# Channel sums of a head pair as f32r passes over high and low halves

## The chip, the cores and the metric

The kernel runs on one core of a Trainium2 chip. The metric is the device time of one execution in microseconds (us); three executions of the kernel before gave 2422.89, 2422.91 and 2429.49 us.

## What is computed

Two layers run one after the other on 256 positions of 2048 channels: a block with a pooling, a long-convolution and a gating mixer and a feed-forward part, and a hybrid layer of banded attention, a recurrent state layer and memory attention. The change lies in the hybrid layer, in sums over channels. Cut to those:

```python
# recurrent layer: 16 heads of 64 channels
kk = heads(k * f(k_k))
kk = kk * lax.rsqrt(jnp.maximum(jnp.sum(kk * kk, axis=-1, keepdims=True), 1e-24))   # keys
...
o = rwkv7_scan(rh, dh, kh, vh, -kk, kk * ah)
mean = jnp.mean(o, axis=-1, keepdims=True)
var = jnp.mean(jnp.square(o - mean), axis=-1, keepdims=True)                         # outputs
o = ((o - mean) * lax.rsqrt(var + GN_EPS)).reshape(bsz, s, B_WIDTH) * f(ln_w) + f(ln_b)
bonus = jnp.sum(rh * kh * f(r_k), axis=-1, keepdims=True) * vh                       # bonus
# banded attention: 8 heads of 128 channels
aq = rms_norm(aq.reshape(bsz, s, A_HEADS, A_HEAD_DIM), a_q_g)                        # queries
ak = rms_norm(ak.reshape(bsz, s, A_HEADS, A_HEAD_DIM), a_k_g)
```

## The kernel before

Activations lie transposed, with channels on the 128 partitions and the 256 positions along the free side. All large weights come as one stream of 736 **units** of 512 KB, through a ring of four buffers. SP loads a unit into `raw`; ACT copies it, rounded to f32r, into `w_hi` (L967, a wait on `unit_used` for the slot, which TensorE gives four units later); DVE writes the rest `raw - w_hi` into `w_lo` (L1391); TensorE (PE) then runs the 24 products of the unit (`unit`, or `part` in this stage): for each of 4 contraction tiles and 2 output tiles `w_hi` by `h_hi`, `w_hi` by `h_lo`, `w_lo` by `h_hi`, each 128x128 by 256 columns. ACT and DVE run their program four units ahead of PE: `units(k)` on them splits the unit that PE will use at `k + 4`. So "PE's unit k" below is the one in `units(k)` of PE, and "the split of k" is what ACT and DVE do in theirs.

The stage that the change touches has eight rounds, one for each group of two recurrent heads and one attention head (a "head pair" below), 16 units a round. In each round PE weaves two things between its units: `heads(k, g)`, which prepares the pair g from the 16 units' results, and `late`, which works off the pair before (a triangular inverse by chunks of 64, four chunk states one after the other, the attention). The first 16 units run `heads` alone, with work of their own (DVE's six `prefix` steps); then a loop of seven iterations runs `late` with `heads`; then `late` runs once more with the queries of the next stage. The order of each engine is written out by hand, and an engine takes its instructions strictly in that order; semaphores with counts tie them.

The sums over channels are products by a matrix of ones on PE in fp32, from buffers of 128x256 fp32 numbers:

- keys and bonus: DVE squares the keys into `sq` and multiplies `rk` at its split of 6 (`keys_ready`); PE multiplies both by `head_ones` behind its unit 9 into bank 7 (`head_sums`); DVE reads them at its split of 9.
- queries and keys of attention: ACT squares bank 0 into `qr` at its split of 11; PE multiplies `qr` (512 columns) by `ones` behind unit 12; ACT takes the root at its split of 12 (L1214).
- outputs: ACT squares the centred outputs into `gsq`; PE multiplies by `head_ones` behind unit 11; ACT takes the root into `groot`, DVE inverts it (L1994) before its split of 12.

Of DVE in `late`, this stretch matters: it writes the state of chunk 2 (`S`), then does the split of 8 with what `heads` has at 8 (`t0`, `k0`, `v`), then the solution `SA` of chunk 3. At the start of the next `late`: the split of 0, eight masked copies, the reciprocal of `qr` (L1908), `qk` (for PE, which multiplies `qk` behind its unit 1).

Of the kernel before, what the change touches and what calls it, by code (L numbers as in the profile page):

```python
# [26 lines left out]
P = 128  # L27
# [140 lines left out]
def build(nc, a):  # L168
    out_ap = a["out"]
    with ExitStack() as ctx:  # L170
# [100 lines left out]
        for n, w in (("pr", 257), ("pk", 257), ("pv", 257), ("t0", 256), ("r", 256), ("k0", 256), ("v", 256),  # L271
                     ("k2", 256), ("kk", 256), ("sq", 256), ("rk", 256), ("bz", 256), ("ep", 260), ("en", 256),
                     ("a_rt", 512)):
            small[n] = place("s_" + n, [P, w], at)
# [79 lines left out]
        free_mem = sem("free_mem")  # L354
        keys_ready = sem("keys_ready")
        head_sums = sem("head_sums")
# [9 lines left out]

        PROJ = [banks[0], banks[1], banks[3], banks[4]]
# [55 lines left out]
        def _(pe):  # L423
# [51 lines left out]
            pe.wait_ge(tab_in, 32)  # L475
            norm_sums(acc)
# [185 lines left out]

            def heads(k, half=None):

                part(k, half)
                if k == 9 and half != 0:
                    pe.wait_ge(keys_ready, n.next("keys"))
                    mm(banks[7][:, 0:T], con_("head_ones"), small["sq"][:, :])
                    mm(banks[7][:, T:2 * T], con_("head_ones"), small["rk"][:, :]).then_inc(head_sums, 1)
                if k == 12:  # L670
                    pe.wait_ge(sums_read, n.next("sums"))
                    pe.wait_ge(qk_squared, n.next("qk"))
                    mm(banks[7][:, :], con_("ones"), qr[:, :, :].rearrange("p s t -> p (s t)")).then_inc(qk_sums, 1)

            def late(units):
# [283 lines left out]
        def _(act):  # L959
# [57 lines left out]
            act.wait_ge(tab_in, 32)  # L1017
            act.activation(spare[:, 0:1], con_("eps6"), ACT.Sqrt)
# [174 lines left out]
            def heads(k, g):  # L1193
# [15 lines left out]
                if k == 11:  # L1209
                    act.activation(qr[:, :, :], p2(0), ACT.Square).then_inc(qk_squared, 1)  # L1210
                    copy(qk[:, :, :], p2(0)).then_inc(bank_read[0], 1)
                if k == 12:
                    act.wait_ge(qk_sums, n.next("qk"))
                    to_dve(act.activation(flat(qr), banks[7][:, :], ACT.Sqrt, bias=con_("eps6"), scale=1.0 / P))  # L1214
                if k == 13:
# [3 lines left out]
                    to_dve(act.activation(small["en"][:, :], cg_, ACT.Exp, scale=rate))  # L1219
                if k == 15:  # L1220
# [12 lines left out]
            def late(units):  # L1233
# [43 lines left out]
                for k in range(12, 16):  # L1277
                    units(k)
# [965 lines left out]
```

## Time and profile before

| what | value |
|---|---|
| median of three runs | 2422.91 us |
| the profiled execution, its own time | 2422.74 us |
| its span, first to last instruction | 2421.0 us |
| PE busy | 2354.3 us, 97% |
| PE weight loads busy | 2295.7 us, 95% |
| DVE busy | 1507.5 us, 62% |
| ACT busy | 1104.7 us, 46% |
| one iteration of the loop of seven | 70.3 us (1410.90 to 1481.20, say) |
| mean granted clock of TensorE | 0.992 |

The profiled execution lies 0.17 us below the median, and 1.7 us of it are outside the span. Each engine's timeline gives start, duration, line, operation and tiles of every instruction, and in brackets how long the engine was idle before it and who ended that. Starts of matmuls are the pace; their durations overlap, so a matmul of 0.28 us may be followed by the next 0.12 us later. In the profile `s_t` is `t0`, `s_k` is `k0` or `k2`, `con` holds the matrices of ones.

### The profile page before, as it was taken

How to read it: one execution, taken by the hardware profiler on the slowest of the kernel's cores; microseconds unless marked ns; L12 is line 12 of the kernel's file. 1: busy time of each engine (PE TensorE's matmuls, PEld its weight loads, DVE VectorE, ACT ScalarE, POOL GpSimd, SP SyncE). 2: the span in 40 equal slices, each digit the busy share in tenths (PEclk: the TensorE clock that was granted, in tenths of full speed). 3: DMA queues.
4: the chain of work that ended last, by engine and by line, in shares of the span. 5: the costliest groups of instructions: out<-in, count | busy, mean ns of one | idle time of the engine just before them, and what ended most of it. 6: DMA issues, size and time to landing. Idle time of an engine off the chain costs nothing.

```text
span 2421.0 us, 54358 instructions
## 1 busy us (share of the span) xinstructions
PE 2354.3 (97%) x21920; PEld 2295.7 (95%) x21920; DVE 1507.5 (62%) x2072; ACT 1104.7 (46%) x1455; POOL 12.8 (1%) x27
## 2 busy tenths in 40 slices
PE   6999999999999999997999999999999999999999
PEld 6898999999999999996899999999989999999999
DVE  6456776666546667667866666776576554555554
ACT  5343445555434555434444444444465444444442
POOL 0000000000000000000000000000000000000000
PEclk9999999999999999998999999999999999999999
DMA  6453555555555555554343334333445365555554
GB/s 231 141 183 114 174 182 188 186 189 185 189 190 186 190 186 186 188 185 143 126 132 109 126 117 135 126 126 128 149 161 170 111 206 186 189 189 185 192 185 162
DMA packets 110235, 401.34 MB, mean 166 GB/s; under 512 B 12378, under 2 KB 12405, under 8 KB 109952
## 3 DMA queue, kind: packets, MB, share of 16 engines
q1 hardware_dynamic: 108000, 390.91, 49.1%
q0 software_dynamic: 2080, 8.06, 1.0%
q8 instruction: 136, 2.23, 0.4%
q14 instruction: 19, 0.16, 0.0%
HBM read 396.81 MB, written 2.10 MB: 165 GB/s over the span
## 4 chain that ended last, share of the span: by engine, by line
PE 93%; DVE 4%; ACT 1%; issue 1%; DMA 0%; DVEq 0%; SPq 0%; ACTq 0%
PE bank L428 93%; ACT w_hi L967 1%; DVE scratch L1440 1%; DVE w_lo L1391 1%; DVE s_k L1440 0%; DMA x<-in_xT 0%; DVE h_lo L1437 0%; DVE cum L1437 0%; DVE S L1443 0%; PE bank L742 0%; DVE ping L1437 0%; DVE s_t L1437 0%; DVE root L1479 0%; DVE acc L1437 0%; PE bank L691 0%
## 5 line engine op out<-in xcount | busy, mean ns | idle before, releaser
L1391 DVE TENSOR_TENSOR w_lo<-raw,w_hi 128x1024 fp32r<-128x1024 f32 x736 | 896.8, 1224 | 783.2 <-ACT w_hi L967 777.9
L967 ACT ACTIVATE w_hi<-raw 128x1024 fp32r<-128x1024 f32 x736 | 778.3, 1060 | 1088.7 <-PE bank L428 1076.5
L428 PE MATMUL bank<-h_hi,w_hi 128*128 128x256 f32 x4016 | 1149.6, 286 | 19.4 <-issue 8.3
L428 PE MATMUL bank<-h_lo,w_hi 128*128 128x256 f32 x4016 | 1125.6, 280 | 0.0
L428 PE MATMUL bank<-h_hi,w_lo 128*128 128x256 f32 x4016 | 1124.2, 280 | 0.0
L428 PEld LDWEIGHTS bank<-h_hi,w_hi 128*128 128x128 f32 x4016 | 759.3, 189 | 34.1 <-issue 14.3
L428 PEld LDWEIGHTS bank<-h_lo,w_hi 128*128 128x128 f32 x4016 | 759.6, 189 | 3.2 <-issue 2.2
L428 PEld LDWEIGHTS bank<-h_hi,w_lo 128*128 128x128 f32 x4016 | 759.1, 189 | 0.0
L428 PE MATMUL bank<-m_hi,w_hi 128*128 128x256 f32 x704 | 196.5, 279 | 0.0
L428 PE MATMUL bank<-m_lo,w_hi 128*128 128x256 f32 x704 | 196.5, 279 | 0.0
L428 PE MATMUL bank<-m_hi,w_lo 128*128 128x256 f32 x704 | 196.5, 279 | 0.0
L428 PEld LDWEIGHTS bank<-m_hi,w_hi 128*128 128x128 f32 x704 | 132.3, 188 | 0.0
L428 PEld LDWEIGHTS bank<-m_lo,w_hi 128*128 128x128 f32 x704 | 132.3, 188 | 0.0
L428 PEld LDWEIGHTS bank<-m_hi,w_lo 128*128 128x128 f32 x704 | 132.3, 188 | 0.0
L428 PE MATMUL bank<-ya_hi,w_hi 128*128 128x256 f32 x384 | 107.1, 279 | 0.0
L428 PE MATMUL bank<-ya_lo,w_hi 128*128 128x256 f32 x384 | 107.1, 279 | 0.0
L428 PE MATMUL bank<-ya_hi,w_lo 128*128 128x256 f32 x384 | 107.1, 279 | 0.0
L1440 DVE SCALAR_TENSOR_TENSOR conv_o<-scaled_up,par,conv_o 128x255 f32<-128x255 f32 x176 | 77.1, 480 | 6.2 <-DVE conv_o L1440 5.9
L428 PE MATMUL bank<-mh_hi,w_hi 128*128 128x256 f32 x256 | 73.8, 288 | 5.4 <-DVE mh_lo L1437 3.4
L428 PEld LDWEIGHTS bank<-ya_hi,w_hi 128*128 128x128 f32 x384 | 72.2, 188 | 0.0
L428 PEld LDWEIGHTS bank<-ya_lo,w_hi 128*128 128x128 f32 x384 | 72.2, 188 | 0.0
L428 PEld LDWEIGHTS bank<-ya_hi,w_lo 128*128 128x128 f32 x384 | 72.2, 188 | 0.0
(404 smaller groups left out, 2712.3 us busy)
## 6 DMA issues: line engine op xcount, KB each, us to landing
raw<-in_units SPq DMA_DIRECT2D x736, 512.0 KB, 3.8
x<-in_xT SPq DMA_DIRECT2D x4, 512.0 KB, 6.0
memx<-in_memT POOLq DMA_DIRECT2D x4, 512.0 KB, 7.9
out_y<-obuf SPq DMA_DIRECT2D x8, 256.0 KB, 4.5
bias_t<-in_bias POOLq DMA_DIRECT2D x8, 192.0 KB, 3.2
dft<-in_dft POOLq DMA_DIRECT2D x1, 1024.0 KB, 7.7
decay<-in_decay POOLq DMA_DIRECT2D x1, 768.0 KB, 5.8
inv<-in_inv POOLq DMA_DIRECT2D x1, 512.0 KB, 3.8
```

Source lines behind the costliest of these rows:

```text
L428: return pe.matmul(out, lhsT, rhs, start=start, stop=stop, skip_group_check=True)
L967: return act.activation(out, in_, ACT.Copy, scale=scale)
L1391: dve.tensor_tensor(w_lo[slot][:, :, :], raw[slot][:, :, :], w_hi[slot][:, :, :].bitcast(F32), ALU.subtract).then_inc(split_done, 1)
L1440: return dve.scalar_tensor_tensor(out, x_, s, y_, op0, op1)
```

## The change

Each of the four sums is made of two f32r products, one over a rounded high half and one over the rest, added in the same bank, by rounded copies of the two matrices of ones (`ones_r`, `head_r`, written once by ACT at the program's start; PE's first product waits for them). What it adds and moves:

- **keys and bonus**: `sq` and `rk` lie side by side (`sqrk`). ACT copies them rounded into `s_hi` at its split of 7, DVE writes `s_lo` right behind its split of 8 and ahead of `t0`, `k0`, `v`, and PE waits for that (`keys_split`) at the same place as before, behind unit 9.
- **queries**: ACT squares bank 0 twice at its split of 11, into `qr` and rounded into `s_hi`; DVE writes `s_lo` behind its split of 12 (`qk_split`); PE's sum moves from behind unit 12 to behind unit 13, ACT's root from its split of 12 to that of 14, behind the exponentials of 13 instead of ahead of them.
- **outputs**: ACT squares twice, into `gsq` and rounded into `g_hi`; DVE writes `g_lo` behind its split of 10; PE's sum moves from behind unit 11 to behind unit 12, and ACT's root and DVE's chain on it (L1994 on) behind the split of 12.

```diff
+        ones_r = place("ones_r", [P, P], 104 * K + 256, F32R)
+        head_r = place("head_r", [P, P], 105 * K + 256, F32R)
+        s_hi = place("s_hi", [P, 2, T], 74 * K, F32R)
+        s_lo = place("s_lo", [P, 2, T], 76 * K, F32R)
...
@@ tensor
+            def two_halves(ones):
+                mm(banks[7][:, :], ones[:, :], s_hi[:, :, :].rearrange("p s t -> p (s t)"), True, False)
+                return mm(banks[7][:, :], ones[:, :], s_lo[:, :, :].rearrange("p s t -> p (s t)"), False, True)
...
                 if k == 9 and half != 0:
-                    pe.wait_ge(keys_ready, n.next("keys"))
-                    mm(banks[7][:, 0:T], con_("head_ones"), small["sq"][:, :])
-                    mm(banks[7][:, T:2 * T], con_("head_ones"), small["rk"][:, :]).then_inc(head_sums, 1)
-                if k == 12:
+                    pe.wait_ge(keys_split, n.next("keys"))
+                    two_halves(head_r).then_inc(head_sums, 1)
+                if k == 13:
                     pe.wait_ge(sums_read, n.next("sums"))
-                    pe.wait_ge(qk_squared, n.next("qk"))
-                    mm(banks[7][:, :], con_("ones"), qr[:, :, :].rearrange("p s t -> p (s t)")).then_inc(qk_sums, 1)
+                    pe.wait_ge(qk_split, n.next("qk"))
+                    two_halves(ones_r).then_inc(qk_sums, 1)
...
                 units(11, 1)
-                from_act()
-                mm(banks[6][:, 0:T], con_("head_ones"), small["gsq"][:, :]).then_inc(psum_for_act, 1)
-                for k in range(12, 16):
+                units(12)
+                from_dve()
+                mm(banks[6][:, 0:T], head_r[:, :], g_hi[:, :], True, False)
+                mm(banks[6][:, 0:T], head_r[:, :], g_lo[:, :], False, True).then_inc(psum_for_act, 1)
+                for k in range(13, 16):
@@ scalar
             act.wait_ge(tab_in, 32)
+            copy(ones_r[:, :], con_("ones"))
+            copy(head_r[:, :], con_("head_ones")).then_inc(ones_rounded, 1)
             act.activation(spare[:, 0:1], con_("eps6"), ACT.Sqrt)
...
                 if k == 7:
                     act.wait_ge(keys_ready, n.next("keys"))
+                    to_dve(copy(s_hi[:, :, :], sqrk[:, :, :]))
...
                 if k == 11:
-                    act.activation(qr[:, :, :], p2(0), ACT.Square).then_inc(qk_squared, 1)
+                    n.next("qk")
+                    act.activation(qr[:, :, :], p2(0), ACT.Square)
+                    act.activation(s_hi[:, :, :], p2(0), ACT.Square).then_inc(qk_squared, 1)
                     copy(qk[:, :, :], p2(0)).then_inc(bank_read[0], 1)
-                if k == 12:
-                    act.wait_ge(qk_sums, n.next("qk"))
-                    to_dve(act.activation(flat(qr), banks[7][:, :], ACT.Sqrt, bias=con_("eps6"), scale=1.0 / P))
                 if k == 13:
...
+                if k == 14:
+                    act.wait_ge(qk_sums, n.now("qk"))
+                    to_dve(act.activation(flat(qr), banks[7][:, :], ACT.Sqrt, bias=con_("eps6"), scale=1.0 / P))
...
-                to_pe(act.activation(small["gsq"][:, :], banks[4][:, 0:T], ACT.Square))
+                act.activation(small["gsq"][:, :], banks[4][:, 0:T], ACT.Square)
+                to_dve(act.activation(g_hi[:, :], banks[4][:, 0:T], ACT.Square))
                 units(11)
+                units(12)
                 psum()
@@ vector
                 if k == 8:
                     from_act()
+                    low(s_lo[:, :, :], sqrk[:, :, :], s_hi[:, :, :]).then_inc(keys_split, 1)
+                    from_act()
                     prev, now = shift("pv")
...
+                if k == 12:
+                    dve.wait_ge(qk_squared, n.next("qk"))
+                    low(s_lo[:, :, :], qr[:, :, :], s_hi[:, :, :]).then_inc(qk_split, 1)
...
                 units(10)
+                from_act()
+                to_pe(low(g_lo[:, :], sm["gsq"][:, :], g_hi[:, :]))
                 units(11)
+                units(12)
```

How this stands on two engines. On DVE, in the loop, from the state of chunk 2 to the solution of chunk 3 (`S`, `SA`; `w_lo` is the split of 8), before:

```order
L1440 SCALAR_TENSOR_TENSOR S<-bank,s_ep,S_dec 64x64
L1391 TENSOR_TENSOR w_lo<-raw,w_hi 128x1024 [waits hi_done]
L1437 TENSOR_TENSOR s_t_128<-s_pv 128x256 [waits act_for_dve]
L1440 SCALAR_TENSOR_TENSOR s_k_130<-s_k_130,bank 128x256
L1440 SCALAR_TENSOR_TENSOR s_v<-s_t_128,par,s_pv 128x256
L1437 TENSOR_TENSOR SA<-bank,m_b_115 64x64 [waits psum_for_dve]
```

and of the change:

```order
L1466 SCALAR_TENSOR_TENSOR S<-bank,s_ep,S_dec 64x64
L1417 TENSOR_TENSOR w_lo<-raw,w_hi 128x1024 [waits hi_done]
L1463 TENSOR_TENSOR s_lo<-s_sqrk,s_hi 128x512 [waits act_for_dve]
L1463 TENSOR_TENSOR s_t_128<-s_pv 128x256 [waits act_for_dve]
L1466 SCALAR_TENSOR_TENSOR s_k_130<-s_k_130,bank 128x256
L1466 SCALAR_TENSOR_TENSOR s_v<-s_t_128,par,s_pv 128x256
L1463 TENSOR_TENSOR SA<-bank,m_b_115 64x64 [waits psum_for_dve]
```

The low half stands behind the split, and all that DVE has up to the solution of chunk 3 moves behind it.

On ACT, in the loop, from the root of the outputs to the end of the iteration (splits of 12 to 15; `avf` and `az` are values and gates of attention), before:

```order
L1275 ACTIVATE s_groot<-bank,con 128x256 [waits psum_for_act]
L967 ACTIVATE w_hi<-raw 128x1024 [waits unit_used]
L1214 ACTIVATE qr<-bank,con 128x512 [waits qk_sums]
L1218 ACT_TABLE_LOAD
L1218 ACTIVATE s_ep<-cum 128x4x64
L1219 ACTIVATE s_en<-cum 128x256
L967 ACTIVATE avf<-bank 128x256 [waits unit_used]
L1222 ACTIVATE az<-bank 128x256
```

and of the change:

```order
L1301 ACTIVATE s_groot<-bank,con 128x256 [waits psum_for_act]
L1239 ACT_TABLE_LOAD
L1239 ACTIVATE s_ep<-cum 128x4x64
L1240 ACTIVATE s_en<-cum 128x256
L986 ACTIVATE w_hi<-raw 128x1024 [waits unit_used]
L1243 ACT_TABLE_LOAD
L1243 ACTIVATE qr<-bank,con 128x512 [waits qk_sums]
L986 ACTIVATE avf<-bank 128x256 [waits unit_used]
L1246 ACT_TABLE_LOAD
L1246 ACTIVATE az<-bank 128x256
```

The root of the queries now stands between the exponentials and the tanh of the gates (`w_hi` rows that only repeat are left out), and the program has a table load ahead of each of the three.

## Rows read from the trace of the kernel before

**Rows 1.** The page's first part: busy time, share of the span, instructions of each engine.

```profile
PE 2354.3 (97%) x21920; PEld 2295.7 (95%) x21920; DVE 1507.5 (62%) x2072; ACT 1104.7 (46%) x1455; POOL 12.8 (1%) x27
```

**Rows 2.** PE's timeline (start, duration, line, operation, [idle before]): keys and bonus.

```profile
1455.58 0.59 PE L428 MATMUL bank<-s_sq,con 128*128 128x256 f32 x2
1456.01 0.59 PE L428 MATMUL bank<-s_rk,con 128*128 128x256 f32 x2
```

**Rows 3.** PE's timeline: last product of unit 11 to second of unit 13.

```profile
1463.54 0.28 PE L428 MATMUL bank<-h_hi,w_lo 128*128 128x256 f32 x1
1463.65 0.59 PE L428 MATMUL bank<-s_gsq,con 128*128 128x256 f32 x2
1464.20 0.28 PE L428 MATMUL bank<-h_lo,w_hi 128*128 128x256 f32 x1
...
1466.80 0.28 PE L428 MATMUL bank<-h_hi,w_lo 128*128 128x256 f32 x1
1466.91 1.02 PE L428 MATMUL bank<-qr,con 128*128 128x512 f32 x2
...
1467.89 0.28 PE L428 MATMUL bank<-h_lo,w_hi 128*128 128x256 f32 x1
```

**Rows 4.** DVE's timeline: a 128x512 addition, a state, the split of 8.

```profile
12.26 0.69 DVE L1437 TENSOR_TENSOR acc<-acc 128x512 f32<-128x512 f32 x1
...
1446.63 0.59 DVE L1443 TENSOR_SCALAR S<-bank,s_ep 64x64 f32<-64x64 f32 x2
...
1454.56 1.23 DVE L1391 TENSOR_TENSOR w_lo<-raw,w_hi 128x1024 fp32r<-128x1024 f32 x1
1455.70 0.42 DVE L1437 TENSOR_TENSOR s_t<-s_pv 128x256 f32<-128x256 f32 x1
```

**Rows 5.** PE's timeline: the product that waited for that state.

```profile
1447.28 0.33 PE L428 MATMUL bank<-S,m_b 64*64 64x64 f32 x4 [1.29 <-DVE S L1443]
```

**Rows 6.** ACT's timeline: splits of 12 to 15 and of 0, roots, gates.

```profile
1467.11 1.06 ACT L967 ACTIVATE w_hi<-raw 128x1024 fp32r<-128x1024 f32 x1 [0.86 <-PE bank L428]
1468.08 0.67 ACT L1214 ACTIVATE qr<-bank,con 128x512 f32<-128x512 f32 x1
...
1470.80 1.06 ACT L967 ACTIVATE w_hi<-raw 128x1024 fp32r<-128x1024 f32 x1 [2.05 <-PE bank L428]
1471.88 1.28 ACT L1218 ACT_TABLE_LOAD   x1
...
1476.45 1.06 ACT L967 ACTIVATE w_hi<-raw 128x1024 fp32r<-128x1024 f32 x1 [1.60 <-PE bank L428]
...
1477.68 0.38 ACT L1222 ACTIVATE az<-bank 128x256 f32<-128x256 f32 x1
1479.28 1.06 ACT L967 ACTIVATE w_hi<-raw 128x1024 fp32r<-128x1024 f32 x1 [1.22 <-PE bank L428]
```

**Rows 7.** DVE's timeline, next iteration: its split of 0, then qk.

```profile
1480.37 1.23 DVE L1391 TENSOR_TENSOR w_lo<-raw,w_hi 128x1024 fp32r<-128x1024 f32 x1 [1.60 <-ACT w_hi L967]
...
1487.67 0.88 DVE L1440 SCALAR_TENSOR_TENSOR qk<-qk,par,qr 128x256 f32<-128x256 f32 x2
```

**Rows 8.** PE's timeline: the product of qk.

```profile
1488.61 0.92 PE L428 MATMUL bank<-qk 128*128 128x128 f32 x4
```

**Rows 9.** DVE's timeline, first 16 units: splits of 8, and of 11 and 12.

```profile
1173.94 1.22 DVE L1391 TENSOR_TENSOR w_lo<-raw,w_hi 128x1024 fp32r<-128x1024 f32 x1
...
1187.90 2.37 DVE L1391 TENSOR_TENSOR w_lo<-raw,w_hi 128x1024 fp32r<-128x1024 f32 x2
```

**Rows 10.** PE's timeline, first 16 units: key sum, query sum, first product of late.

```profile
1169.75 0.59 PE L428 MATMUL bank<-s_sq,con 128*128 128x256 f32 x2
...
1182.93 2.05 PE L428 MATMUL bank<-qr,con 128*128 128x512 f32 x2 [3.75 <-ACT qr L1210]
...
1198.04 0.32 PE L428 MATMUL bank<-s_a_rt,m_b 64*64 64x128 f32 x1
```

**Rows 11.** Busy time by stretch (length, engines, granted clock, DMA): behind the query sum's wait.

```profile
1184.00:1188.00 4.00, 4.00 (x18) 3.48 (x17) 3.90 (x6) 0.90 (x2) 0.00 (x0) 0.50 0.40 131
```

More of the change, by code:

```diff
@@ L273, in build @@
                      ("a_rt", 512)):
-            small[n] = place("s_" + n, [P, w], at)
+            if n == "sq":
+                sqrk = place("s_sqrk", [P, 2, T], at)
+                small["sq"], small["rk"] = sqrk[:, 0, :], sqrk[:, 1, :]
+            elif n != "rk":
+                small[n] = place("s_" + n, [P, w], at)
             at += (4 * w + 31) // 32 * 32
@@ L354, in build @@
         free_mem = sem("free_mem")
+        ones_rounded = sem("ones_rounded")
         keys_ready = sem("keys_ready")
+        keys_split = sem("keys_split")
+        qk_split = sem("qk_split")
         head_sums = sem("head_sums")
@@ L365, in build @@
         stored = sem("stored")
+        ones_r = place("ones_r", [P, P], 104 * K + 256, F32R)
+        head_r = place("head_r", [P, P], 105 * K + 256, F32R)
+        s_hi = place("s_hi", [P, 2, T], 74 * K, F32R)
+        s_lo = place("s_lo", [P, 2, T], 76 * K, F32R)
+        g_hi = place("g_hi", [P, T], 57 * K, F32R)
+        g_lo = place("g_lo", [P, T], 59 * K, F32R)
         PROJ = [banks[0], banks[1], banks[3], banks[4]]
@@ L475, in _ @@
             pe.wait_ge(tab_in, 32)
+            pe.wait_ge(ones_rounded, 1)
             norm_sums(acc)
@@ L1276, in late @@
                                       scale=1.0 / 64))
-                for k in range(12, 16):
+                for k in range(13, 16):
                     units(k)
@@ L1874, in heads @@
                     step(dve.tensor_copy(sm["bz"][:, :], sm["k0"][:, :]))
-                    from_act(2)
+                    from_act()
                     step(stt(a_rt[:, :, 0, :], c4(sm["kk"][:, :]), -1.0, ep4[:, :, 0:CHUNK], ALU.mult, ALU.mult))
@@ L1904, in late @@
                 settle()
-                from_act()
+                from_act(2)
                 read(stt(az[:, :], az[:, :], 1.0, p2(1)[:, 1, :], ALU.add, ALU.mult), 1)
@@ L1990, in late @@
                 units(10)
+                from_act()
+                to_pe(low(g_lo[:, :], sm["gsq"][:, :], g_hi[:, :]))
                 units(11)
+                units(12)
                 from_act()
@@ L2003, in late @@
                 step(stt(y_tile(g + 8), sm["gk"][:, :], 0.5, sm["bz"][:, :], ALU.mult, ALU.mult))
-                for k in range(12, 16):
+                for k in range(13, 16):
                     units(k)
@@ L2017, in _ @@
                     to_act(dve.memset(ep4[:, :, 0:1], 1.0))
-            with n.loop(HEADS_A - 1, {"unit": 16, "psum": 16, "act": 7, "step": 47, "to_pe": 16, "to_act": 3,
-                                      ("fill", 0): 2, ("fill", 1): 2, "bias": 1, "keys": 1, "sums": 1}) as i:
+            with n.loop(HEADS_A - 1, {"unit": 16, "psum": 16, "act": 9, "step": 47, "to_pe": 17, "to_act": 3,
+                                      ("fill", 0): 2, ("fill", 1): 2, "bias": 1, "keys": 1, "sums": 1, "qk": 1}) as i:
                 late(lambda k: heads(k, i + 1), i)
```

## The prediction

> **What bounds the kernel now.** I read the busy shares first. PE is busy for 97% of the span, DVE and ACT far less [rows 1]. So a shorter product on PE shortens the kernel where nothing makes PE wait, and work added to DVE and ACT is free only where PE is not about to wait for it. PE's timeline gives the pace: 22 products from 1464.20 to 1466.80 [rows 3], 0.118 us each, so 2.83 us for the 24 of a unit. At that pace almost any delay of PE is a delay of the end. Then I looked, for each of the four sums, at who will give PE its operands after the change and when, on the timelines of DVE and ACT. A second reading is where PE already hangs on DVE with nothing to spare: the product of `qk` starts at 1488.61 [rows 8], 0.06 us after DVE has ended `qk` at 1487.67 + 0.88 [rows 7]. The same 0.06 us lies between the state's end, 1446.63 + 0.59 [rows 4], and the product that waited 1.29 us for it [rows 5]. So 0.06 us is the hand-over from DVE to PE, and the product of `qk` is one that DVE releases, though no long wait shows there.
>
> **What PE saves.** The fp32 product of the keys takes 0.43 us (1455.58 to 1456.01 [rows 2]), the bonus another, 0.86 together. The outputs: from the last product of unit 11 to the second of unit 12 it is 0.66 us [rows 3], less two paces (0.24) gives 0.42. The queries: 1466.91 to 1467.89 less one pace [rows 3] gives 0.86. In place of these stand f32r products. 256 columns cost one pace, 0.118; for 512 the trace has no f32r row. From above it is two paces, 0.24; from below a quarter of the fp32 product of 512 columns, 0.215, if fp32 makes four passes of what f32r makes one. I take 0.225, in the middle, as the ends are close: 0.45 for a pair. So a round saves 0.41 on keys and bonus, 0.41 on the queries, and 0.42 - 0.24 = 0.18 on the outputs: **1.0 us**, and eight rounds 8.0 us. If no wait came with it, that would be all.
>
> **The keys' low half comes too late.** DVE starts its split of 8 at 1454.56 and its next instruction at 1455.70, so 1.14 later [rows 4]. PE starts the key sum at 1455.58 [rows 2], before that. Until now it could, since its operands were made two splits earlier; now `s_lo` is that next instruction. A 128x512 addition takes 0.69 us [rows 4]; from below half the split's pace, 0.57, from above 0.75, should f32r output or two sources side by side cost a little. I take 0.69. `s_lo` ends at 1456.39, PE starts at 1456.45: a **wait of 0.87 us** in each iteration (0.75 to 0.93). It can't close by itself: the split of 8 stands behind the state of chunk 2, for which DVE waits for PE, so both shift together. ACT's copy `s_hi` is early (its split of 7 is some 8 us before). Behind the waiting sum on PE are the solution of chunk 3 and unit 10. On DVE `SA` of chunk 3 comes 0.69 later, and PE wants it only behind unit 10, 2.83 us on; that stays hidden.
>
> **The other two low halves.** `g_lo` of the outputs: DVE writes it at the end of its split of 10, ACT's `g_hi` being ready by then, and PE now asks a whole unit later than before; I count no wait. The queries: at the end of unit 12 PE stands 0.0 us from where it stood (0.87 - 0.41 - 0.42 of the sum that went from ahead of unit 12 to behind it). From unit 12's last product to ACT's split it is 0.31 (1466.80 [rows 3] to 1467.11 [rows 6]), to DVE's 1.09 more (1479.28 [rows 6] to 1480.37 [rows 7]), then 1.14, `s_lo` 0.69 and the hand-over 0.06: 3.29 us. PE has one pace, the outputs' two products (0.24) and unit 13 (2.83) to do: 3.19. **Wait 0.1 us** (0 to 0.2). DVE's chain on `groot` now comes behind this, and the operands of `late` behind that chain; PE asks for them three units after the query sum (8.5 us), so I hold that hidden.
>
> **Two more table loads on ACT.** The root of the queries moves between the exponentials and the tanh: a table load ahead of it and one ahead of the gates `az`. A load takes 1.28 us and starts 1.08 behind the start of a split [rows 6]. Split of 14, load, root (next one 0.57 after its start, as instructions start 0.1 before the one ahead ends: 0.67 [rows 6]): 1.08 + 1.29 + 0.57 = 2.94 us to the split of 15, against PE's 2.83: 0.11 late. Split of 15, `avf` (0.97 behind, as the root was behind a split: 1467.11 to 1468.08), load, `az`: 0.97 + 0.38 + 1.29 + 0.28 = 2.92 to the split of 0: another 0.09. Before, ACT had been idle for 1.22 us there [rows 6]. The split of 0 is what DVE waits for, and from it runs an unbroken chain to `qk`, 1480.37 to 1488.55 [rows 7], which PE takes up 0.06 later [rows 8]. So the 0.2 us arrive on PE: **0.2 us a round** (0 to 0.4), eight times.
>
> The row shows 1.28 us for a load, begun 0.02 after the split ahead of it has ended (1470.80 + 1.06 [rows 6]). The Trainium skill ("ScalarE: Activation LUTs", What ACT_TABLE_LOAD costs) counts a drain of about 1.38 us on top, 2.66 us a switch. By that, an estimate from the page, the two loads would put the split of 0 some 3 us late instead of 0.2. I go by the row, which has no such gap.
>
> **The loop.** Saved 1.0, waits 0.87 + 0.1 + 0.2 = 1.17: **+0.17 us** an iteration, seven times +1.2. The last `late` has only the outputs' gain and the wait at `qk`: -0.18 + 0.2 = 0.
>
> **The first 16 units.** Here DVE is the one that is late, with the prefix steps between its splits. PE reaches the key sum at 1169.75 [rows 10]; DVE comes to its split of 8 at 1173.94 [rows 9], `s_lo` starts at 1175.08 and PE gets it at 1175.83: a wait of 6.1 us where there was none. The old wait of 3.75 us ahead of the query sum [rows 10] is not added to that, as DVE's chain goes on. Its splits of 11 and 12 were at 1187.90 [rows 9]; pushed by the first `s_lo` they run from 1188.59 to 1190.87, the second `s_lo` to 1191.56, and PE starts the query sum, now behind unit 13, at 1191.62. Then 0.45 and units 14, 15 and the first of `late` (8.49) and 0.09 of change-over: the first product of `late` at 1200.65, against 1198.04 [rows 10]: **+2.6 us**. The clock: after the 3.75 us the granted clock was 0.50, 1.2 GHz [rows 11]. After a wait of 6.1 us it will be again. The key sum and unit 10 at half rate take 6.0 us to 1181.8, units 11 to 13 end at 1190.3, still before 1191.62. So it costs nothing unless it lasts for over half a unit more.
>
> **Start of the program.** Two 128x128 copies on ACT, together less than one 128x512 root [rows 6], while DVE still adds up the squares (0.69 us of it at 12.26 [rows 4]) and PE has yet to sum them: nothing.
>
> **Sum.** 1.2 + 0 + 2.6 = +3.8 us on the profiled execution's own 2422.74, whose distance to the median is 0.2: **2426.6 us**, 0.16% slower, which is no change that can be told. A measurement of this kernel tells about 0.3%, 7.3 us: 2415.6 to 2430.2 counts as the same.
>
> **Rivals.**
>
> *All of the gain.* The low half of the keys is there in time and the clock is kept: -8.0 us, and perhaps part of the old 3.75 us, 2412 to 2415. For it speaks that PE is the bound and that the rest is plain arithmetic; against it that PE's start lies 0.12 us before even the beginning of `s_lo`, in the order as written. Chance 0.05.
>
> *A part of it.* `s_lo` shorter than taken, ACT's 0.2 us swallowed, f32r of 512 columns at 0.215: the loop gains 0.2 us an iteration instead of losing, 2422 to 2424. Chance 0.15; the same verdict.
>
> *The clock in the first 16 units, on the other side.* PE stands for 6.1 us, then again at the query sum. If the clock comes back soon, PE reaches that sum early, at about 1188.8, and stands for nearly 3 us; after 3.75 us the clock fell. A second fall at half rate over two units, as [rows 11] show for one, costs +2.5 to +3.5 us; a first one that lasts a unit longer, +1 to +2.8. It decides for slower from +3.6 over my sum: 2430 to 2433. Chance 0.1.
>
> *A table load with its drain.* If each of the two added loads costs 1.38 us more, the split of 0 is 2.9 us late and `qk` with it: 8 x 2.8 = 22 us, 2449 us. The rows speak against it. That is the page's rule named above. Chance 0.03.
>
> *The passes don't get shorter.* If an f32r product of 512 columns took 0.43 us, the change would not do what it says: nothing saved on keys and queries, +6.6 us on the forecast, 2433. The units' products of 256 columns at 0.118 speak against it. Chance 0.03.
>
> **How the numbers follow.** The forecast, waits that take back the gain of the loop and a longer first stretch, has 0.64, and its own bounds (key wait 0.75 to 0.93, query wait 0 to 0.2, ACT 0 to 0.4, all times seven or eight) give 2424 to 2429.5. The range takes in the partial gain and most of the clock's case: 2421.5 to 2432. Faster by over 0.3%: 0.06 (the full gain, and a little of things not seen). Slower: 0.1 + 0.03 + 0.03 and 0.02 of the forecast's upper end, 0.18. The same: 0.76.
>
> **What would show it.** In the profile after: PE's key sum with a wait of 0.8 to 0.9 us for DVE's `s_lo` in each of seven iterations, and of about 6 us in the first; the query sum some 0.1 us behind unit 13's pace; ACT's split of 0 without idle time before it; four table loads a round; an iteration of 70.4 to 70.6 us instead of 70.3; the first product of `late` near 1200.6. The prediction is wrong if the key sum starts without a wait (then it is some 7 us faster), if the first stretch ends beyond 1203 (clock), or if a place I held hidden (`SA` of chunk 3, the centred outputs, the operands of `late`) shows as a wait of PE.

## The result and the profile after

The changed kernel takes 2430.1 us (median of 20 runs), the kernel before, run beside it, 2423.9 us (20 runs): a ratio of 1.0023, with a 95% interval of 1.0013 to 1.0032, so about 5.6 us (3.2 to 7.8) slower. 2426.6 us with a range of 2421.5 to 2432.0 had been forecast, and "the same" as the likeliest verdict. The sign of the small loss was right; its size is some 2 us more than the sum had.

The profiled execution of the changed kernel took 2428.62 us, with a span of 2427.0. Its page, against [rows 1]:

```profile
PE 2349.3 (97%) x21904; PEld 2291.6 (94%) x21904; DVE 1517.8 (63%) x2096; ACT 1136.8 (47%) x1497; POOL 12.8 (1%) x27
```

PE is busy 5.0 us less and the span is 6.0 us longer: PE now stands for 11 us more. The waits of PE from the recurrent layer on to the end of the stage (engine, line, who was waited for: us in total, times, longest), after:

```profile
PE bank L441 <- DVE s_lo L1463: 12.5, 9, 5.9
PE bank L441 <- DVE S L1469: 9.0, 7, 1.3
PE bank L441 <- ACT icl L1316: 1.6, 1, 1.6
PE bank L441 <- DVE qk L1466: 1.6, 8, 0.3
```

The wait for the state `S` is the old one, seven times 1.29 [rows 5]. The one for the queries' root, 3.75 [rows 10], has gone. `s_lo`, the low half, is new: once 5.9, once 1.7, and seven times 0.7. And `qk`, behind which no long wait showed before [rows 8], now shows eight times.

**Where the 6 us are.** Three marks cut the span: the first product of the low-rank part at the start of the stage (`lt`), the first product of `late` (`s_a_rt,m_b`), and the last product of the column sums just behind the stage (`csq`). Each is a row of a tile's view:

```profile
L441 PE MATMUL bank<-lt,lora x32: 376/376/481, 1138.8 to 1151.8; 64*128 64x256 f32 x32
L441 PE MATMUL bank<-s_a_rt,m_b x128: 269/269/320, 1199.0 to 1696.0; 64*64 64x128 f32 x128
L441 PE MATMUL bank<-csq,con x16: 377/379/379, 1764.2 to 1801.9; 128*128 128x256 f32 x16
```

| us | `lt` first | to the first of `late` | an iteration of the loop | `lt` to the last `csq` | timed ratio |
|---|---|---|---|---|---|
| before | 1140.5 | 57.5 | 70.28 | 657.3 | 1 |
| after | 1138.8 | 60.2 | 70.75 | 663.1 | 1.0023 |

The iteration is a mean over six, from one waiting product of `S` to the next (1237.68 to 1662.18 after, 1236.43 to 1658.11 before). Ahead of the stage, where the change adds only the two small copies at the start, the changed kernel was 1.7 us early; with the same copies the other profiled kernels came to `lt` between 1139.1 and 1140.4. Behind the stage 1.9 us were lost, some 1.5 of them to a clock of 0.97 from 1800 to 1850, where it was 1.00 before. Nothing is changed there, and e9 below needs no more than the kernel before from the last `csq` to the first product of `ya_hi` (138.4 and 138.3 us; the changed kernel 140.2). So I count neither as the change's. The stage itself accounts for it: +5.8 us, beside the 5.6 us of the timed runs. Of them 2.7 are in the first 16 units and 7 x 0.47 = 3.3 in the loop; behind the loop 0.2 come back.

**In the loop**, PE's timeline at the key sum, after, where [rows 2] stood:

```profile
1459.10 0.50 PE L441 MATMUL bank<-s_hi,head_r 128*128 128x512 f32 x1 [0.70 <-DVE s_lo L1463]
1459.43 0.40 PE L441 MATMUL bank<-s_lo,head_r 128*128 128x512 f32 x1
1459.76 0.33 PE L441 MATMUL bank<-S,m_b 64*64 64x64 f32 x4
```

and DVE's, where [rows 4] stood:

```profile
1457.21 1.23 DVE L1417 TENSOR_TENSOR w_lo<-raw,w_hi 128x1024 fp32r<-128x1024 f32 x1
1458.36 0.68 DVE L1463 TENSOR_TENSOR s_lo<-s_sqrk,s_hi 128x512 fp32r<-128x512 f32 x1
```

The low half begins 1.15 behind its split, lasts 0.68, and PE starts 0.06 after it. From the product of `S` that waited (1449.93 and 1447.28 [rows 5]) to the key sum it is 9.17 us, 8.30 before [rows 2]: +0.87, what was forecast. (The 0.70 in brackets is less, since it counts only from the end of the record ahead, and records overlap.) But the pair then takes 0.33 and 0.33 to the next product.

At the query sum, after, against [rows 3]:

```profile
1472.60 0.28 PE L441 MATMUL bank<-h_hi,w_lo 128*128 128x256 f32 x1
1472.95 0.47 PE L441 MATMUL bank<-s_hi,ones_r 128*128 128x512 f32 x1
1473.26 0.40 PE L441 MATMUL bank<-s_lo,ones_r 128*128 128x512 f32 x1
1473.49 0.28 PE L441 MATMUL bank<-h_hi,w_hi 128*128 128x256 f32 x1
```

0.35 between the last product of unit 13 and the sum, less a pace of 0.12: a wait of 0.23 that is not in brackets, since the records of the products overlap.

ACT's timeline from behind its split of 14 to that of 0, against [rows 6]:

```profile
1477.58 1.28 ACT L1243 ACT_TABLE_LOAD   x1
1478.87 0.69 ACT L1243 ACTIVATE qr<-bank,con 128x512 f32<-128x512 f32 x1
1479.46 1.05 ACT L986 ACTIVATE w_hi<-raw 128x1024 fp32r<-128x1024 f32 x1
1480.41 0.37 ACT L986 ACTIVATE avf<-bank 128x256 f32<-128x256 f32 x1
1480.80 1.28 ACT L1246 ACT_TABLE_LOAD   x1
1482.09 0.38 ACT L1246 ACTIVATE az<-bank 128x256 f32<-128x256 f32 x1
1482.37 1.05 ACT L986 ACTIVATE w_hi<-raw 128x1024 fp32r<-128x1024 f32 x1
```

No row has idle time in front: the 1.22 us ahead of the split of 0 [rows 6] are used up, and `qk` comes late for PE, where [rows 8] stood without a wait:

```profile
1491.69 0.92 PE L441 MATMUL bank<-qk 128*128 128x128 f32 x4 [0.20 <-DVE qk L1466]
```

**In the first 16 units** PE's timeline and the stretches behind the wait (length, busy time of PE, PE's weight loads, DVE, ACT and GpSimd, granted clock, DMA), against [rows 10] and [rows 11]:

```profile
1174.12 0.79 PE L441 MATMUL bank<-s_hi,head_r 128*128 128x512 f32 x1 [5.91 <-DVE s_lo L1463]
...
1189.93 0.47 PE L441 MATMUL bank<-s_hi,ones_r 128*128 128x512 f32 x1 [1.69 <-DVE s_lo L1463]
```

```profile
1172.00:1176.00 4.00, 1.88 (x7) 1.69 (x8) 3.97 (x8) 0.00 (x0) 0.00 (x0) 0.52 0.56 199
1176.00:1180.00 4.00, 4.00 (x24) 4.00 (x24) 3.97 (x6) 0.47 (x2) 0.00 (x0) 0.63 0.11 38
1180.00:1184.00 4.00, 4.00 (x36) 4.00 (x35) 3.96 (x4) 2.26 (x3) 0.00 (x0) 1.00 0.42 157
```

The clock falls to its lower level (about 0.5, 1.2 GHz) behind the 5.9 us, and is back before 1180; PE still reaches the query sum 1.7 us before its operand.

### The profile page after: what moved, and what is told of

Its sections match the earlier page's. It is cut to its first block, busy times and chain, and to the rows that moved or that the text cites. A ratio compares the mean times of both kernels' runs of the same rounds, so it can differ in the third digit from the quotient of the medians.

```text
span 2427.0 us, 54406 instructions
## 1 busy us (share of the span) xinstructions
PE 2349.3 (97%) x21904; PEld 2291.6 (94%) x21904; DVE 1517.8 (63%) x2096; ACT 1136.8 (47%) x1497; POOL 12.8 (1%) x27
## 4 chain that ended last, share of the span: by engine, by line
PE 87%; DVE 7%; issue 3%; ACT 3%; DMA 0%; DVEq 0%; SPq 0%; ACTq 0%
PE bank L441 87%; ACT w_hi L986 1%; DVE qr L1939 1%; DVE w_lo L1417 1%; DVE scratch L1466 1%; ACT L1246 0%; ACT L1243 0%; DVE s_k L1466 0%; DMA x<-in_xT 0%; DVE h_lo L1463 0%; DVE s_lo L1463 0%; DVE cum L1463 0%; DVE ping L1463 0%; DVE qk L1466 0%; DVE S L1469 0%
## 5 line engine op out<-in xcount | busy, mean ns | idle before, releaser
L441 PE MATMUL bank<-mh_lo,w_hi 128*128 128x256 f32 x256 | 72.3, 282 | 0.0
```

The lines of the kernel that those rows point to most:

```text
L441: return pe.matmul(out, lhsT, rhs, start=start, stop=stop, skip_group_check=True)
```

## Experiments

Each run is read by the same columns as above. An iteration is the same in all six of a run to within 0.1 us, so it tells more than the time of one execution does: executions of the kernel before lay between 2419.9 and 2433.8 us. e1 to e3 were executed once (2430.2, 2431.7, 2428.4 us) and are read by their iteration and stage alone: e1 and e2 lost 4.7 us in a stretch behind the stage (last section), more than either edit is worth.

| us | to the first of `late` | iteration | `lt` to the last `csq` | timed ratio |
|---|---|---|---|---|
| before | 57.5 | 70.28 | 657.3 | 1 |
| after | 60.2 | 70.75 | 663.1 | 1.0023 (1.0013 to 1.0032) |
| e1 keys ahead | 60.2 | 70.20 | 659.1 | |
| e2 queries ahead | 59.0 | 70.47 | 659.9 | |
| e3 root at 13 | 60.6 | 70.52 | 661.6 | |
| e4 all three | 59.0 | 69.66 | 654.0 | 1.0005 (0.9992 to 1.0018) |
| e5 first 16 in fp32 | 54.4 | 70.75 | 661.4 | 1.0013 (1.0004 to 1.0023) |
| e6 e4 and e5 | 56.0 | 69.66 | 651.0 | 0.9970 (0.9958 to 0.9982) |
| e7 before, sum moved | 54.5 | 70.27 | 654.5 | 0.9990 (0.9981 to 0.9999) |
| e8 e4 with fp32 products | 60.9 | 70.31 | 660.8 | 1.0013 (1.0003 to 1.0022) |
| e9 e6, outputs ahead | 54.4 | 69.48 | 648.4 | 0.9965 (0.9952 to 0.9978) |

### The low half of the keys ahead of the split

The edits of e1 to e3 are each made to the changed kernel.

```diff
             def heads(k, g):     # DVE
+                if k == 8:
+                    from_act()
+                    low(s_lo[:, :, :], sqrk[:, :, :], s_hi[:, :, :]).then_inc(keys_split, 1)
                 split()
...
                 if k == 8:
                     from_act()
-                    low(s_lo[:, :, :], sqrk[:, :, :], s_hi[:, :, :]).then_inc(keys_split, 1)
-                    from_act()
```

> The change with one edit: DVE writes the keys' low half ahead of its split of 8 instead of behind it. My theory, that the wait of 0.86 us at the key sum is owed to that place alone: the low half is ready some 0.4 us before PE asks, the wait is gone in all seven iterations, an iteration falls from 70.72 to 69.9 us, and the whole by about 6 us. In the first 16 units the wait of PE at the key sum falls from 5.9 to about 4.8 us, but the first product of late stays where it was, as DVE's chain sets it. The rival, that PE waits for something else as soon as this wait is gone (the solution of chunk 3, the centred outputs): an iteration stays at 70.5 to 70.7 us and the wait shows at the next product that DVE or ACT releases. A second question: behind the wait the two f32r products of 512 columns took 0.33 and 0.23 us (without the 0.1 us that a change to the small fp32 products costs in either kernel). If it is the wait that makes the first one slow, it falls to about 0.22 here; if a product of 512 columns always costs that, it stays at 0.33.

Measured: the iteration falls by 0.55, to 70.20. PE's key sum, without a wait in the loop:

```profile
1457.34 0.28 PE L441 MATMUL bank<-h_hi,w_lo 128*128 128x256 f32 x1
1457.46 0.40 PE L441 MATMUL bank<-s_hi,head_r 128*128 128x512 f32 x1
1457.69 0.40 PE L441 MATMUL bank<-s_lo,head_r 128*128 128x512 f32 x1
1458.02 0.33 PE L441 MATMUL bank<-S,m_b 64*64 64x64 f32 x4
```

It follows that the wait was owed to the place of the low half on DVE, and more: the pair now takes 0.56 where it took 0.66, so the first f32r product behind a wait had cost 0.10 on top. The gain of 0.97 wasn't kept, though, and an iteration of 69.9 had been expected. A wait that neither kernel had stands in the waits view:

```profile
PE bank L441 <- ACT s_o L986: 1.5, 7, 0.2
```

PE comes earlier to the centred outputs, and ACT has the copies `s_o` behind its split of 10. The 0.2 is only what shows in brackets. From the unit's product ahead of the place to the second behind it, it is 1.15 us here:

```profile
1463.17 0.27 PE L441 MATMUL bank<-h_hi,w_lo 128*128 128x256 f32 x1
1464.32 0.28 PE L441 MATMUL bank<-h_lo,w_hi 128*128 128x256 f32 x1
```

In the changed kernel, and in the one before, it is 0.67 (1464.93 to 1465.60, 1461.69 to 1462.36). So 0.48 are lost there, and 0.97 - 0.48 = 0.49 is near the 0.55 measured.

### The low half of the queries ahead of the split

```diff
             def heads(k, g):     # DVE
+                if k == 12:
+                    dve.wait_ge(qk_squared, n.next("qk"))
+                    low(s_lo[:, :, :], qr[:, :, :], s_hi[:, :, :]).then_inc(qk_split, 1)
                 split()
...
-                if k == 12:
-                    dve.wait_ge(qk_squared, n.next("qk"))
-                    low(s_lo[:, :, :], qr[:, :, :], s_hi[:, :, :]).then_inc(qk_split, 1)
```

> The change with one edit: DVE writes the queries' low half ahead of its split of 12, where it was idle for 1.45 us, instead of behind it. My theory: the wait of 0.23 us at the query sum goes, an iteration falls from 70.72 to about 70.5 us, and in the first 16 units, where DVE is the late one, the low half comes one split (1.14 us) earlier, so that the first product of late stands 1.1 us less far behind the low-rank products that begin the stage. The rival, that DVE's split of 12 is then late and holds up PE instead: an iteration is no shorter, with a wait for w_lo or s_lo elsewhere.

Measured: the iteration falls by 0.28, the first 16 units by 1.2; the query sum starts without a wait in the loop. So the query wait was real and worth 0.28, not 0.1.

### The root of the queries ahead of the exponentials

```diff
                 if k == 13:     # ACT
+                    act.wait_ge(qk_sums, n.now("qk"))
+                    to_dve(act.activation(flat(qr), banks[7][:, :], ACT.Sqrt, bias=con_("eps6"), scale=1.0 / P))
                     cg_ = ...
-                if k == 14:
-                    act.wait_ge(qk_sums, n.now("qk"))
-                    to_dve(act.activation(flat(qr), banks[7][:, :], ACT.Sqrt, bias=con_("eps6"), scale=1.0 / P))
```

DVE's counts of what it waits for from ACT move with it.

> The change with one edit: ACT takes the queries' root at its split of 13 ahead of the exponentials, with the table for roots still loaded, instead of at 14 between exponentials and tanh. My theory: two table loads a round go (16 of the whole), the split of 0 is no longer behind them, and the wait of 0.23 us at the product of qk is gone: an iteration of about 70.5 us against 70.72. The rival, that the exponentials, now 0.6 us later, hold up the operands of late: a wait of PE for m_b or s_a_rt, and an iteration of 70.7 us or more.

Measured: the iteration falls by 0.23. Table loads of an iteration go from four to two, the wait for `qk` is gone from the list, and ACT is idle again ahead of its split of 0:

```profile
1481.16 0.38 ACT L1245 ACTIVATE az<-bank 128x256 f32<-128x256 f32 x1
1482.72 1.06 ACT L986 ACTIVATE w_hi<-raw 128x1024 fp32r<-128x1024 f32 x1 [1.19 <-PE bank L441]
```

So two table loads cost 2.56 us of ACT's time and 0.23 us of the kernel's, the part that didn't fit in ACT's idle time.

### All three

The three edits above together.

> The three edits together. My theory: all three waits are gone, an iteration of 69.35 to 69.5 us (before: 70.28; the change: 70.72), seven times 0.9 less than before; the first 16 units still 1.3 to 1.6 us longer than before. Together 4.5 to 5.5 us below the kernel before, a ratio of 0.998. The rival, that the f32r products are no gain worth the work on DVE and ACT: a ratio of 1.000 or more, with new waits of PE in the loop.

Measured: an iteration of 69.66, 1.09 less than the changed kernel; the sum of the three is 1.06, so they add: the three waits stand behind one another, and none hides another. The stage is 3.3 us shorter than that of the kernel before. The timed ratio, 1.0005, does not show these 3.3 us; its interval reaches to 0.9992, 2 us faster, so the expected 0.998 was missed, as was an iteration of 69.35 to 69.5. The profiled execution (2419.83 us) lies near the low end of its 12 runs (2419.4 to 2432.7). What the other executions lost, no trace here tells. In the loop only the waits for `S` and `s_o` are left.

### Products alone

The kernel with all three edits; high and low halves are still made.

```diff
-                    two_halves(head_r).then_inc(head_sums, 1)
+                    mm(banks[7][:, :], con_("head_ones"), sqrk[:, :, :].rearrange("p s t -> p (s t)")).then_inc(head_sums, 1)
...
-                    two_halves(ones_r).then_inc(qk_sums, 1)
+                    mm(banks[7][:, :], con_("ones"), qr[:, :, :].rearrange("p s t -> p (s t)")).then_inc(qk_sums, 1)
...
-                mm(banks[6][:, 0:T], head_r[:, :], g_hi[:, :], True, False)
-                mm(banks[6][:, 0:T], head_r[:, :], g_lo[:, :], False, True).then_inc(psum_for_act, 1)
+                mm(banks[6][:, 0:T], con_("head_ones"), small["gsq"][:, :]).then_inc(psum_for_act, 1)
```

> The kernel with the three moves, all high and low halves made as there, but PE makes each of the sums by one fp32 product of the whole numbers at the same place. So it measures what the shorter products alone are worth where nothing waits for them. By the prediction's terms 0.41 + 0.41 + 0.18 = 1.0 us a round: the loop from 489.3 to 496.3 us. By the pairs as they stood in the changed kernel, where the first product behind a wait took 0.33 in place of 0.23 us, 0.3 + 0.3 + 0.18 = 0.8 us a round: 494.8 us. If the products were hidden behind other waits anyway, under 492.

Measured: 70.31 against 69.66, 0.65 an iteration; the loop from the first to the last product of `late` is 493.9 us, between "hidden" (under 492) and the lower of the two sums (494.8). The places themselves say why. The key sum of this kernel, and that of e4:

```profile
1457.63 1.02 PE L441 MATMUL bank<-s_sqrk,con 128*128 128x512 f32 x2
1458.58 0.33 PE L441 MATMUL bank<-S,m_b 64*64 64x64 f32 x4
```

```profile
1454.18 0.39 PE L441 MATMUL bank<-s_hi,head_r 128*128 128x512 f32 x1
1454.42 0.40 PE L441 MATMUL bank<-s_lo,head_r 128*128 128x512 f32 x1
1454.74 0.27 PE L441 MATMUL bank<-S,m_b 64*64 64x64 f32 x2
```

0.95 to the next product against 0.56: 0.39 saved. The queries in the same way, 0.98 against 0.59: 0.39. The outputs, 0.55 against 0.35: 0.20. Together **0.98 us**, the 1.0 of the prediction. Of these, 0.65 arrive. What is missing is the wait for `s_o`, which e4 has and this slower kernel hardly has. PE at the centred outputs here, then in e4:

```profile
1463.76 0.28 PE L441 MATMUL bank<-h_hi,w_lo 128*128 128x256 f32 x1
1463.88 0.66 PE L441 MATMUL bank<-s_o,con 128*128 128x256 f32 x2
1464.18 0.47 PE L441 MATMUL bank<-h_hi,w_hi 128*128 128x256 f32 x1
1464.49 0.28 PE L441 MATMUL bank<-h_lo,w_hi 128*128 128x256 f32 x1
```

```profile
1459.89 0.28 PE L441 MATMUL bank<-h_hi,w_lo 128*128 128x256 f32 x1
1460.36 0.70 PE L441 MATMUL bank<-s_o,con 128*128 128x256 f32 x2 [0.18 <-ACT s_o L986]
...
1461.01 0.28 PE L441 MATMUL bank<-h_lo,w_hi 128*128 128x256 f32 x1
```

0.73 from the unit's product to the second of the next half here, 1.12 there: 0.39 lost. (Where nothing waits it is 0.67, as in the changed kernel, so e4 loses 0.45 there in all.) 0.98 - 0.39 = 0.59, near the 0.65 measured. Neither of the two sums of the expectation had this; both took the saving as kept whole.

### The first 16 units without halves

In the first 16 units `heads` is called with `first=True`:

```diff
-                    pe.wait_ge(keys_split, n.next("keys"))
-                    two_halves(head_r).then_inc(head_sums, 1)
+                    pe.wait_ge(keys_ready if first else keys_split, n.next("keys"))
+                    if first:
+                        mm(banks[7][:, :], con_("head_ones"), sqrk[:, :, :].rearrange("p s t -> p (s t)")).then_inc(head_sums, 1)
+                    else:
+                        two_halves(head_r).then_inc(head_sums, 1)
```

and so for the queries; ACT makes no `s_hi` and DVE no `s_lo` there; a one-column instruction in place of each keeps the semaphore counts.

> The change, but in the first 16 units (once in the program) the two sums are single fp32 products again and neither high nor low halves are made there; the query sum stays behind unit 13. My theory: DVE's low half behind its split of 8 and nothing else makes PE stand 5.9 us at the key sum, and DVE's chain sets the rest. Without it the key sum starts without a wait, the query sum stands 0 to 1 us for the square (which it had stood 3.75 us for, one unit earlier), and unit 15 is what waits for DVE's split of 11, 1 to 2.5 us. First product of late 55 to 57.5 us behind the first lora product, in place of 60.2 (changed kernel) and 57.5 (before). The loop stays at 497.0 us (first to last state product), the time 3 to 5 us below the changed kernel's: 2425 to 2427. Rival: the clock falls behind another wait and the first stretch takes 59 to 60 us all the same; then the time stays within 1.5 us of the changed kernel's.

Measured: the first product of `late` comes 5.8 us sooner, at 54.4, so `s_lo` was what PE stood for. But of these 5.8 only 1.7 reach the end of the stage, and the time, 2428.4 us, isn't the 2425 to 2427 expected. PE now comes so early to the first `late` that it waits there, for ACT's chain with its three table loads and DVE behind it. PE's timeline, then the stretch behind:

```profile
1200.49 0.27 PE L441 MATMUL bank<-m_N,m_Nt 64*64 64x64 f32 x1 [0.66 <-DVE m_No L1475]
...
1206.12 0.92 PE L441 MATMUL bank<-qk 128*128 128x128 f32 x4 [1.96 <-DVE qk L1478]
```

```profile
1208.00:1212.00 4.00, 4.00 (x40) 3.86 (x40) 1.04 (x5) 0.56 (x1) 0.55 (x1) 0.63 0.64 184
```

0.7 and 1.8 us of waits (1.96, of which the changed kernel has 0.2), and a clock at 0.63 for four microseconds (some 1.5), where the changed kernel has 1.00: 4 of the 5.8 are given back. e9 below shows that it is the table loads: it comes to the first `late` at the same 54.4, with the root of the queries at 13 and so one load on ACT from the split of 13 on in place of three. There `qk` is done 9.7 us behind the first product of `late` in place of 12.4, PE waits 0.25 us for it, and the clock stays at 1.00. I had named only the first stretch; a gain there is kept only where the next place has slack, and it had none.

### The kernel before with its query sum moved

```diff
             def heads(k, half=None):     # PE
...
-                if k == 12:
+                if k == 13:
                     pe.wait_ge(sums_read, n.next("sums"))
...
             def heads(k, g):     # ACT
-                if k == 12:
+                if k == 13:
                     act.wait_ge(qk_sums, n.next("qk"))
                     to_dve(act.activation(flat(qr), banks[7][:, :], ACT.Sqrt, bias=con_("eps6"), scale=1.0 / P))
-                if k == 13:
                     cg_ = ...
```

> The kernel before with nothing but the query sum's place changed: PE's fp32 sum behind unit 13 in place of 12, ACT's root at its split of 13 ahead of the exponentials. It tells how much of the gain of the improved version is from f32r passes at all. If the move alone does it, the first stretch falls from 57.5 to 54.5 to 56 us and the loop stays at 493.7 us: 1.5 to 3 us faster, ratio 0.9985 to 0.9995. If the wait of 3.75 us only moves to unit 15 with the clock, the first stretch stays at 57.5 and the ratio is 1.000.

Measured: 54.5 in the first stretch, 70.27 in the loop, the stage 2.8 us shorter, ratio 0.9990. The 3.75 us wait [rows 10] became one of 0.2 us for the squares, and one of 0.6 and one of 2.35 us for the splits, and the clock of [rows 11] stayed at 1.00. Here, with two table loads less than e5 on ACT ahead of the first `late`, nothing was given back. So nearly 3 us of what the changed kernel's order can bring has nothing to do with f32r.

### All three with the first 16 units in fp32

The edits of e4 and e5 together.

> The three moves of the run before (low half of the keys ahead of the split of 8, low half of the queries ahead of the split of 12, root of the queries at the split of 13) and fp32 sums without halves in the first 16 units. The two parts touch different stretches, so they should add: loop 489.3 us as with the three moves (before 493.7), first product of late 55 to 57.5 us behind the first lora product. Stage from the first lora product to the end of the last late 650 to 652 us against 657.3 of the kernel before: 5 to 7 us faster, a ratio of 0.997 to 0.998. Rival: what the stage saves is lost behind it (weights not yet there, the clock), ratio 0.999 to 1.001.

Measured: the stage takes 651.0 us, 6.3 less than before, and the ratio is 0.9970, both as expected. Against the changed kernel the stage is 12.1 us shorter, more than the 9.1 of e4 and the 1.7 of e5 together, since the place that took back most of e5's gain has slack here. (The timed ratios of e4 and e5 would give 0.9995; most of the 2.5 thousandths between are what e4's stage gained and its times didn't show, and that stays open.) Against e7, which moves the sum alone, the stage is 3.5 us shorter: 4.6 from the first to the last product of `late` (489.4 against 494.0) and 0.4 behind it, less 1.5 in the first stretch, where the clock fell in this run and not in e7 (last section). So the f32r passes bring some 4 to 5 of the 7 us that seven rounds of 1.0 offer.

### The outputs ahead of the split

On top of e6.

```diff
-                for k in range(7, 11):     # ACT, late
+                for k in range(7, 10):
                     units(k)
                 from_dve()
                 psum()
                 copy(small["o"][HALVES[0], :], banks[OUT[0]][HALVES[0], 0:T])
                 to_pe(copy(small["o"][HALVES[1], :], banks[OUT[1]][HALVES[1], 0:T]))
+                units(10)
```

> The three moves with fp32 sums in the first 16 units, and one more: ACT copies the outputs (s_o) ahead of its split of 10 in place of behind it. In the loop of that kernel PE stood at the product of the centred outputs, 1459.89 to 1461.01 for what took 0.73 us where nothing waited (the kernel with fp32 products in the same places): 0.39 us an iteration. If ACT's split of 10 was what held s_o, the loop falls by 7 x 0.39 = 2.7 us, from 489.4 to 486.7, the wait for s_o is gone, and the ratio to the kernel before is 0.995 to 0.997. If s_o is late because of the root of the keys' sums ahead of that split, 0 to 1 us. If the split of 10, now 0.75 us later, makes DVE and with it g_lo late, a wait for g_lo stands in its place and nothing is gained.

Measured: the wait for `s_o` is gone, the iteration falls by 0.18 (69.66 to 69.48), not by 0.39: the third case came in for half. The split of 10 is later on ACT, DVE's `g_lo` behind it too, ready at 1460.51, and PE meets it:

```profile
1460.28 0.28 PE L441 MATMUL bank<-h_hi,w_lo 128*128 128x256 f32 x1
1460.56 0.39 PE L441 MATMUL bank<-g_hi,head_r 128*128 128x256 f32 x1
1460.79 0.28 PE L441 MATMUL bank<-g_lo,head_r 128*128 128x256 f32 x1
1460.90 0.28 PE L441 MATMUL bank<-h_hi,w_hi 128*128 128x256 f32 x1
```

0.62 over three starts that are 0.35 apart in all where nothing waits: 0.27 lost. The place of the centred outputs takes 0.67 again (1455.61 to 1456.28), 0.45 less than in e4, and 0.45 - 0.27 = 0.18 is what was measured. This version has the lowest median: 2417.0 us, ratio 0.9965 (0.9952 to 0.9978), the stage 8.9 us shorter than before. The timed ratios don't tell it from e6, and of the 2.6 us by which its stage is shorter than that of e6, 1.6 are the clock in the first stretch and not this edit.

## The prediction, point by point

- **PE saves 1.0 us a round**: right, 0.98 (0.39 + 0.39 + 0.20) in e8 against e4. The f32r product of 512 columns, which no row of before showed, has a pace of 0.23 to 0.24 us, inside the bounds of 0.215 and 0.24.
- **Key wait of 0.87**: right, +0.87, and it was removed by moving the low half alone (e1). What the step left out is that the first product behind a wait takes 0.33 in place of 0.23: +0.10.
- **Query wait of 0.1**: too small, 0.23, and another 0.07 in the pair behind it; e2 gives 0.28 back. It was the difference of two chains of about 3.2 us, 3.29 and 3.19, and its bounds of 0 to 0.2 were those of one row, not of a difference. Most of the miss is the hand-over, taken as 0.06 and measured as 0.14 (last section).
- **0.2 at `qk` for two table loads**: right, 0.20 to 0.23 (e3 gives 0.23), and the loads have no time around them beyond their 1.28 us. The Trainium skill's drain of about 1.38 us a switch ("ScalarE: Activation LUTs", What ACT_TABLE_LOAD costs) isn't there: 1477.58 + 1.28 is 1478.86 and the root starts at 1478.87.
- **The loop +0.17 an iteration**: +0.47, an iteration of 70.75 where 70.4 to 70.6 had been named as the sign. From the places: 0.87 + 0.10 + 0.23 + 0.07 + 0.23 - 0.98 = 0.52. The failed step is the size of this term, by 0.10 for the keys' first product and 0.20 for the queries'; 7 x 0.3 = 2.1 us is the whole difference between the forecast's 3.8 and the measured 5.6 to 5.8. (On 2422.74 the terms sum to 2426.7, not 2426.6.)
- **The first 16 units +2.6**: right, 60.2 against 57.5. The wait was 5.91 us (6.1 forecast), the clock fell to 0.52 and cost nothing, as worked out, since DVE was what PE waited for next (1.69 us at the query sum). The rival that the clock falls a second time didn't happen: the granted clock behind the 1.69 us is 1.00. But it was near: in e8 PE stands 1.87 us at the same place, the clock behind is 0.76 and 0.81 over eight microseconds, and the first stretch takes 60.9 us against e4's 59.0.
- **Held hidden**: `SA` of chunk 3, the centred outputs, the operands of `late`, the copies at the start: none shows as a wait in the changed kernel. The centred outputs have little slack: with PE 0.97 us earlier they cost 0.48 (e1), so it is some 0.5 us.
- **Rivals**: the full gain and the part of it fell with the key wait; the passes are shorter; the table load has no drain.
- **The verdict**: "the same" had been counted up to 2430.2 us, and the median of 2430.1 is just inside, which is luck. Of its 3.5 us above the forecast 1.2 are the kernel before itself (2423.9 in 20 runs, 2422.7 in the sum). And "no change that can be told" was too strong: the interval of 20 runs, 3.2 to 7.8 us, does tell the loss from nothing.

The chances would have been better spread upwards: the misses of 0.1 us and more all went the same way, each being a cost of a hand-over that had been left out.

## To carry to other kernels

A product made shorter is worth its time only where its operands come as early as before. Write the low half ahead of the long instruction of its engine, not behind it, and then read the waits again, since the next operand in the order (here `s_o`, then `g_lo`) had been hidden by the time just saved. Of 1.0 us a round saved on PE, 0.8 arrived in the best version and less than nothing in the plain one. And price the reordering by itself on the old kernel: nearly a third of the best version's gain was that (2.8 of 8.9 us).

## What the runs showed of the hardware

- **A product behind a wait costs 0.1 us more than its pace.** The f32r product of 512 columns: 0.33 to the next start behind a wait (1459.10 to 1459.43, 1472.95 to 1473.26 with 0.31), 0.23 without (1457.46 to 1457.69). That of 256 columns in e9: 0.23 (1460.56 to 1460.79) against 0.12. Why is not shown.
- **The hand-over from DVE to PE is not one number.** 0.06 us at the keys (1458.36 + 0.68 to 1459.10) and 0.14 at the queries (1472.12 + 0.69 to 1472.95); 0.14 or 0.15 there in every iteration, in e1 and e3 too. At the queries the program has PE wait on two semaphores in a row; that this is the cause wasn't tested.
- **The same wait may or may not bring the clock down.** A wait of 2.35 us at unit 15 is in e5, e6, e7 and e9. The granted clock just behind it was 0.64 in e6 (first row) and 1.00 in e7 (second):

```profile
1188.00:1192.00 4.00, 3.82 (x21) 3.82 (x22) 3.02 (x8) 3.79 (x6) 0.00 (x0) 0.64 0.59 165
```

```profile
1188.00:1192.00 4.00, 2.92 (x25) 2.92 (x26) 3.80 (x6) 2.90 (x3) 0.00 (x0) 1.00 0.42 131
```

  That is the 1.6 us between e6 (56.0) and e9 (54.4) in the first stretch; e5 and e9 have 1.00 there too. Nor does the length of the one wait decide it: the clock fell behind 1.87 us in e8 and not behind 2.52 us in e1 (1.00 from 1188 on). What decides it stays open.
- **A pace that differs between executions.** Behind 1930 us, where no kernel was changed, the products of 256 columns had a median of 279 ns in the profiled executions of before, after, e3, e4, e5 and e7 (280 for `ya_hi` in e5 and e7), and of 281 ns in e1, e2, e6, e8 and e9. From the first product of `ya_hi` to the last of `mg_hi` that makes 481.2 us (1936.1 to 2417.3 before) and 485.8 (1940.5 to 2426.3 in e2): some 4.7 us, as much as most of the edits here bring. Ahead of the stage, over `m_hi`, all eleven have 279 or 280. Each kernel was profiled once, so whether it goes with the kernel or with the execution was not settled. It is why the kernels here are compared by the stage and not by the time of the profiled execution.
